# A two-block fp32 network on one core: 32 more tokens by row gathers, dense expert units of 352 columns, and smaller matrices in norms, scores and block inverse

## What is computed

```python
q = (xb @ w_q).reshape(p, PEER_HEADS, 2, PEER_DK_HALF)            # 8 heads, 2 halves of 64
sc = jnp.einsum('phcd,hcnd->phcn', q, sub_keys)                   # 128 keys for each half
top_s, top_i = lax.top_k(sc, PEER_TOPK)                           # 16 of 128, twice
cand_s = (top_s[:, :, 0, :, None] + top_s[:, :, 1, None, :]).reshape(p, PEER_HEADS, kk)
best_s, best_pos = lax.top_k(cand_s, PEER_TOPK)                   # 16 experts for each head
g = jax.nn.softmax(best_s, axis=-1)
act = jax.nn.gelu(jnp.einsum('phkd,pd->phk', expert_u[idx], xb))  # idx: 128 experts for a token
return jnp.einsum('phk,phkd->pd', g * act, expert_v[idx])         # 16384 experts in all
```

## Time and profile before

| | us |
|---|---|
| median of three runs | 1985.86 (1983.73 to 1988.62) |
| the profiled execution | 1983.03 |
| its span, first to last instruction | 1981.3 |
| PE busy | 1834.3 (93%) |
| DVE busy | 1620.6 (82%) |
| POOL busy | 1054.1 (53%) |
| ACT busy | 708.5 (36%) |
| moved by the DMA engines | 440.34 MB |

### The profile page before, as it was taken

One profiled execution on the slowest core, in us unless ns is written; L12 is line 12 of the kernel. 1 busy time (PEld: TensorE's weight loads), 2 busy tenths in 40 slices (PEclk: granted clock), 3 DMA queues, 4 the chain that ended last, 5 costly groups with the idle time before them and its releaser, 6 DMA issues.

```text
span 1981.3 us, 27281 instructions
## 1 busy us (share of the span) xinstructions
PE 1834.3 (93%) x9487; PEld 1581.7 (80%) x9487; DVE 1620.6 (82%) x2566; ACT 708.5 (36%) x1097; POOL 1054.1 (53%) x654
## 2 busy tenths in 40 slices
PE   3997779999999999999999999999999998989885
PEld 1775557999999899999988887878887776778764
DVE  6979967978988798888489999999998868747656
ACT  2343123333333444444333333333334333324441
POOL 1333225488888655555567776767765542343101
PEclk8999779999999999999999999999999999999988
DMA  8241342499889789888999999999994222200011
GB/s 344 88 159 64 128 149 74 137 315 315 308 314 314 258 280 325 300 308 299 317 348 356 353 356 353 349 356 351 363 352 146 75 77 63 73 12 1 2 55 52
DMA packets 160805, 440.34 MB, mean 222 GB/s; under 512 B 13648, under 2 KB 63952, under 8 KB 157648
## 3 DMA queue, kind: packets, MB, share of 16 engines
q1 hardware_dynamic: 65296, 254.71, 36.7%
q0 software_dynamic: 36864, 134.23, 17.9%
q10 hardware_dynamic: 58560, 50.34, 7.7%
HBM read 386.80 MB, written 52.43 MB: 222 GB/s over the span
## 4 chain that ended last, share of the span: by engine, by line
PE 68%; DVE 18%; issue 4%; POOL 4%; ACT 3%; DMA 2%; ACTq 0%; SPq 0%; DVEq 0%; POOLq 0%; PEldq 0%
PE PS L911 30%; PE PS L1078 24%; PE PS L1041 4%; PE PS L1104 4%; POOL w_lo L804 3%; DVE arena L1676 2%; DVE arena L1635 2%; DVE arena L1842 1%; ACT w_hi L1277 1%; PE PS L926 1%; POOL arena L852 1%; PE PS L1002 1%; DMA arena<-in_expert_u_rows,arena 1%; DMA xres<-in_x 1%; DVE arena L1774 1%
## 5 line engine op out<-in xcount | busy, mean ns | idle before, releaser
L804 POOL TENSOR_TENSOR w_lo<-raw,w_hi 128x1024 fp32r<-128x1024 f32 x300 | 725.0, 2417 | 757.7 <-ACT w_hi L1277 756.5
L1277 ACT ACTIVATE w_hi<-raw 128x1024 fp32r<-128x1024 f32 x332 | 351.9, 1060 | 973.4 <-PE PS L911 609.7
L911 PE MATMUL PS<-act_hi,w_hi 128*128 128x384 f32 (+1 forms) x1632 | 603.9, 370 | 37.3 <-DVE act_lo L1648 12.2
L911 PE MATMUL PS<-act_hi,w_lo 128*128 128x384 f32 (+1 forms) x1632 | 588.4, 361 | 0.0
L911 PE MATMUL PS<-act_lo,w_hi 128*128 128x384 f32 (+1 forms) x1632 | 587.5, 360 | 0.0
L911 PEld LDWEIGHTS PS<-act_hi,w_hi 128*128 128x128 f32 x1632 | 311.8, 191 | 91.7 <-issue 25.3
L911 PEld LDWEIGHTS PS<-act_lo,w_hi 128*128 128x128 f32 x1632 | 312.0, 191 | 26.4
L911 PEld LDWEIGHTS PS<-act_hi,w_lo 128*128 128x128 f32 x1632 | 312.6, 192 | 24.3 <-issue 1.4
L1078 PE MATMUL PS<-w_hi,act_hi 128*128 128x512 f32 x768 | 301.3, 392 | 5.6 <-ACT arena L1398 3.0
L1078 PE MATMUL PS<-w_lo,act_hi 128*128 128x512 f32 x768 | 300.2, 391 | 0.0
L1078 PE MATMUL PS<-w_hi,act_lo 128*128 128x512 f32 x768 | 299.9, 390 | 0.0
(11 more groups left out here) (317 smaller groups left out, 1962.7 us busy)
## 6 DMA issues: line engine op xcount, KB each, us to landing
raw<-in_expert_u SPq DMA_DIRECT2D x128, 512.0 KB
raw<-in_expert_v SPq DMA_DIRECT2D x128, 512.0 KB
raw<-in_w_in SPq DMA_DIRECT2D x52, 512.0 KB
arena<-in_w_ada SPq DMA_DIRECT2D x24, 1024.0 KB, 7.1
gel_d<-arena ACTq DMA_DIRECT2D x64, 384.0 KB
gates_d<-arena ACTq DMA_DIRECT2D x12, 2048.0 KB
arena<-gates_d SPq DMA_DIRECT2D x32, 768.0 KB, 7.1
arena<-gel_d SPq DMA_DIRECT2D x32, 768.0 KB
```

The costliest lines, as they stand in the source:

```text
L804: pool.tensor_tensor(w_lo[:, k % SPLIT, :], raw[:, k % RAW, :], w_hi[:, k % SPLIT, :].bitcast(F32), ALU.subtract).then_inc(lo_split, 1)
L911: mm = pe.matmul(PS[:, bank, 0:n_tok], w[:, k % SPLIT, c * P:(c + 1) * P], x[:, c, 0:n_tok], start=(i == 0 and n == 0), stop=(i == KC - 1 ...
L1277: act.activation(w_hi[:, k % SPLIT, :], raw[:, k % RAW, :], ACT.Copy).then_inc(hi_split, 1)
```

## The change

Constants: `TD` = 384 stays for routing and the V stage, the dense units of the U stage have `TU` = 352 columns. The last 32 tokens of block 2 (`XT`) gather too: each stands on four partitions (`REP`), 32 fetches (`XS`) bring its 128 rows, and 32 row dots give `xdots`. Their gelu is multiplied into the routing weight of these tokens, and the V stage's gelu columns for them are ones. `N1`, `N2` become 82 and 126, the dots in the first part 76, those in the second 52 and 32. `own_ps` is overwritten with the 32 tokens' values at group 44 (`SWAP`), when the first 128 dots are done.

```diff
-TB_ORDER = (3, 0, 1, 2)
+TB_ORDER = (3, 2, 0, 1)
+REP = 4
+XT = P // REP
+XS = SLOTS // REP
+TU = TD - XT
+US = SLOTS + XS
...
-        N1 = 75
-        N2 = 122
+        N1 = 82
+        N2 = 126
...
-        DOTS_A, DOTS_B = 72, 51
+        DOTS_A, DOTS_B = 76, 52
+        SWAP, GELU = 44, 86
...
-        DOTS_IN_U = [(TD // GROUP) * d // DOTS_B for d in range(DOTS_B)]
+        DOTS_IN_U = [SWAP * d // DOTS_B for d in range(DOTS_B)] + [SWAP + 3 + (GELU - SWAP - 4) * d // XS for d in range(XS)]
...
-                linear(U_EU + u, u, u % 2, n_tok=TD)
+                linear(U_EU + u, u, u % 2, n_tok=TU)
...
                 for g in GATES_IN[k]:
+                    if g == SWAP:
+
+                        pe.wait_ge(hsum_ready, 2)
+                        pe.wait_ge(rows_used, SLOTS)
+                        for c in range(KC):
+                            mm = pe.transpose(PS[:, 6 + c // 4, (c % 4) * P:(c % 4 + 1) * P], hsum2[:, c, :], ident[:, :])
+                        mm.then_inc(htok_ps, 1)
                     gate_group(g)
```

The one-hot matrices are made by one comparison of 128x512 and four operations of 128x128 with two scalars, in place of 128x1024 and 128x512. The gelus of the dots move from unit 126 to group 86:

```diff
-                chain.link(v.tensor_tensor(hot[:, n, :, :],
-                                           numbers.unsqueeze(1).unsqueeze(1).to_broadcast([P, GROUP, 2, P]),
...
-                v.tensor_tensor(hot[:, n, 1, :], hot[:, n, 1, :],
-                                weight_ps[:, at].unsqueeze(2).to_broadcast([P, GROUP, P]), ALU.mult).then_inc(hot_ready, 1)
+                chain.post(v.tensor_tensor(hot[:, n, 0, :], numbers.unsqueeze(1).to_broadcast([P, GROUP, P]),
+                                           routeT[:, 0, at].unsqueeze(2).to_broadcast([P, GROUP, P]), ALU.is_equal))
+                for i in range(GROUP):
+                    t = GROUP * g + i
+                    chain.post(v.tensor_scalar(hot[:, t % ONEHOT, 1, :], numbers, routeT[:, 1, t:t + 1], routeT[:, 2, t:t + 1],
+                                               ALU.is_equal, ALU.mult))
```

Scores: keys without zeros, one matmul for each half of 64 rows, four in the q units and twelve behind the first twelve (`N0`) units of the U stage:

```diff
-                    mm = pe.matmul(PS[:, 3 + n % 2, 256 * e:256 * e + 256], qT[:, 2 * hp + e, tb * P:(tb + 1) * P],
-                                   keys[:, 2 * hp + e, :], start=True, stop=True)
+                    for c in range(2):
+                        own = slice(64 * c, 64 * c + 64)
+                        mm = pe.matmul(PS[:, 3 + c, P * e:P * e + P], qT[own, 2 * hp + e, tb * P:(tb + 1) * P],
+                                       keys[own, 2 * hp + e, :], start=True, stop=True)
...
+            for u in range(N0):
+                if u >= 2:
+                    pe.wait_ge(gelu_done, u - 1)
+                linear(U_EU + u, u, u % 2, n_tok=TU)
+                scores(len(SCORED_AFTER) + u)
```

Head norms: the squares' sums come out as 128 tokens x 8, the root and the reciprocal are taken there, ACT spreads the result to 64 columns for each head, and PE turns it back:

```diff
+            def head_sum(i):
...
+                for q in range(TB):
+                    mm = pe.matmul(PS[:, 6 + index % 2, 2 * q:2 * q + 2], sq[:, n % 2, q * P:(q + 1) * P], pair,
+                                   start=True, stop=True)
...
+            def head_spread(i):
...
+                for q in range(TB):
+                    mm = pe.matmul(PS[:, 3 + i % 2, q * P:(q + 1) * P], tmp[:, i % 2, q * P:(q + 1) * P], ident[:, :],
+                                   start=True, stop=True)
...
+                v.reciprocal(hinv[:, i % 2, :], hrms[:, i % 2, :]).then_inc(rinv_ready, 1)
```

In `ada`, PE takes the second four of the eight chunks of parts 2 and 3 (16 matmuls of one column each), parts 4 and 5 come later in DVE's and PE's lists, and the first convolution keeps its partial sums on PSUM:

```diff
-        ADA_AFTER = {3: 4, 5: 5, U_OUT + 1: 6, U_OUT + 2: 7, U_OUT + 3: 8, U_OUT + 4: 9, U_Q + 2: 10, U_Q + 4: 11}
+        PE_SHARE = (2, 3)
+        ADA_AFTER = {5: 4, 7: 5, U_OUT + 1: 6, U_OUT + 2: 7, U_OUT + 3: 8, U_OUT + 4: 9, U_Q + 2: 10, U_Q + 4: 11}
...
-                for c in range(KC):
+                for c in range(4 if h in PE_SHARE else KC):
...
-                    pe.wait_ge(xc_ready, g + 1)
+                    pe.wait_ge(xc_ready, (2, 4, 4, 4)[g])
```

Block inverse: D and its transpose are kept as two diagonal blocks of 64x64 for each head, levels 0 to 5 work on these alone, and the last level joins them. The masks go to 24:

```diff
+            def quarters(name, *pieces):
+
+                b = bank(*name)
+                wait_free(pe, *name)
+                for h in range(GH):
+                    for to, lhs, rhs in pieces:
+                        mm = pe.matmul(PS[to, b, 64 * h:64 * h + 64], lhs[:, h, :], rhs[:, h, :], start=True, stop=True)
                 full(mm, *name)
...
-                    chain.post(v.tensor_tensor(DTm[:, tb, :], DTm[:, tb, :], PS[:, bank("xt", n, tb), :], ALU.subtract))
...
+                        chain.post(v.tensor_tensor(dt, dt, turned_x, ALU.subtract))
...
-                        chain.post(v.tensor_tensor(Dm[:, tb, :], Dm[:, tb, :], PS[:, bank("x", n, tb), :], ALU.subtract))
+                        chain.post(v.tensor_tensor(d, d, PS[:, bank("x", n, tb), 0:256], ALU.subtract))
```

More of the change, by code:

```diff
@@ L465, in build @@
         rows_known = sem("rows_known")
-        rows_got = [sem(f"rows_got{i}") for i in range(RING + 2)]
+        rows_got = [sem(f"rows_got{i}") for i in range(RING)]
         rows_used = sem("rows_used")
@@ L550, in unit_bank, with piece_used @@
             return n % 4 if n < 12 else n % 2 if n < 32 else (n + 1) % 2
+        def piece_used(i):
+            if i % 2 and i // 2 in PE_SHARE:
+                return ada_used_pe, PE_SHARE.index(i // 2) + 1
+            return ada_used, sum(1 for n in range(i + 1) if not (n % 2 and n // 2 in PE_SHARE))
         def cvp(n):
@@ L972, in _ @@
                     if Y_SUM[i] == u:
-                        squares(8 + i, 1, 1 + i, halves)
-            for i in range(8):
-                if Y_SUM[i] == 20:
-                    squares(8 + i, 1, 1 + i, halves)
+                        head_sum(i)
+                    if Y_SPREAD[i] == u:
+                        head_spread(i)
+            head_spread(3)
+            head_sum(6)
+            head_spread(4)
+            head_sum(7)
+            for i in range(5, 8):
+                head_spread(i)
             for c in range(8):
@@ L1015, in _ @@
                     scores(SCORED_AFTER[c])
-            pe.wait_ge(q_sb, 8)
-            for n in range(len(SCORED_AFTER), TB * 4):
-                scores(n)
             pe.wait_ge(hsum_ready, 1)
@@ L1341, in _ @@
                     if Y_SUM[i] == u:
-                        root(1 + i, 64)
+                        head_root(i)
+                    if Y_SPREAD[i] == u:
+                        spread(i)
                 for i in range(8):
@@ L1357, in _ @@
             square(15, y[:, Y_ORDER[7], :])
-            for i in range(5):
-                y_upper(i)
-            root(7, 64)
-            y_upper(5)
-            root(8, 64)
-            y_upper(6)
-            y_upper(7)
+            spread(3)
+            y_upper(0)
+            y_upper(1)
+            head_root(6)
+            spread(4)
+            y_upper(2)
+            head_root(7)
+            spread(5)
+            y_upper(3)
+            spread(6)
+            y_upper(4)
+            spread(7)
+            for i in range(5, 8):
+                y_upper(i)
             for c in range(8):
@@ L1374, in score_copy @@
                 act.wait_ge(score_ps, n + 1)
-                act.activation(S[:, 4 * n:4 * n + 4, :].rearrange("p a b -> p (a b)"), PS[:, 3 + n % 2, :],
-                               ACT.Copy).then_inc(score_sb, 1)
+                own = S[:, 4 * n:4 * n + 4, :].rearrange("p (e c) b -> p e c b", c=2)
+                for c in range(2):
+                    ins = act.activation(own[:, :, c, :], PS[:, 3 + c, 0:2 * P].rearrange("p (e b) -> p e b", e=2), ACT.Copy)
+                ins.then_inc(score_sb, 1)
             for c in range(8):
@@ L1383, in _ @@
                     score_copy(SCORED_AFTER[c])
-            for n in range(len(SCORED_AFTER), TB * 4):
-                score_copy(n)
             def expert_act(u, k, r=None, first=False):
@@ L1695, in _ @@
             chain.link(v.tensor_tensor(ada[:, 0:16], PS[:, 5, 0:16], col("bada", 0, 16), ALU.add))
+            chain.link(v.tensor_tensor(ada[:, 8:16], PS[:, 5, 48:56], ada[:, 8:16], ALU.add))
             chain.link(v.scalar_tensor_tensor(out=gain1, in0=ada[:, 8:16], scalar=1.0, in1=col("n1", 0, 8),
@@ L1927, in _ @@
                     dve.wait_ge(htok_ps, 1)
+                if tb == GT - 1:
+                    own = slice(P - XT, P)
+                    f = row_f[own, :]
+                    chain.link(v.tensor_scalar(f, routed_sb[tb][own, 1, :], float(N_KEYS), None, ALU.mult))
+                    chain.link(v.tensor_tensor(f, f, routed_sb[tb][own, 0, :], ALU.add))
+                    for r in range(REP):
+                        chain.post(v.tensor_copy(row_x[XT * r:XT * r + XT, :], f[:, XS * r:XS * r + XS]))
+                    chain.wait()
+                    dve.nop().then_inc(rows_known, 1)
             assert place == [POINTS, DOTS_A]
```

290 lines of the change are left out of this document (199 added, 91 removed).

## The result

The changed kernel takes 2025.0 us (median of 4 runs, 2021.1 to 2028.2), the kernel before 1985.6 in runs beside it: 1.0196 of it, with an interval of 1.0169 to 1.0222. It is slower by 39 us where 51 us faster was forecast. The forecast put the first U unit at 306, the first routing transposes of PE (which the gate part begins with) at 643, the last group at 923 and the V stage at 953; they came at 339.1, 697.4, 1009.8 and 1042.3 us. So 33 us were lost ahead of the U stage, 22 in its first part, some 32 in the gate part and 2 behind it.

The account below looks back on a forecast made before the run. PE bounds the U and V stages and inverse, with DMA engines and DVE close; DVE bounds the front. -34 -1 -2 +0 -14 = -51: 1932 us profiled, 1935 against the median; own range 1922 to 1948, 8 in 10 within 1905 to 1960.

Parts of the forecast that it names:

- Gate part: U stage's second part: 280 us against 282.2 before, set by DMA work, with about 2 us won.
- a one-hot group is 0.60 for 512 elements and 4 x 0.27: Gate part, DVE's need: 1.7 us a group, with 84 dots of 1.2 in all 264 us.
- the DMA engines' 279.4 us of work: Gate part: raw loads, gathers, gelu and gate stores sum to 279.4 us, more than PE's time, so they set it.
- First part: U stage's first part: units of 3.84 us, with scores and POOL's delays 336.5 us; net gain 1 with scores.
- Front: Everything ahead of the U stage: 34 us won by fewer reciprocals and ada multiply-adds on DVE, ends 24 to 39.
- The later ends it: Front: the later of DVE's bound 181.5 and PE's unit 19 at 165 plus 13 us tail, 178; 35 won.
- hides behind DVE's reciprocal: Front: PE's share of ada, 32 one-column matmuls, costs nothing, so PE's first unit starts 6.4 us earlier.
- Scores: Scores ahead of and in the U stage: 0.63 us each in place of 0.92; 12 behind U units cost 7.6.
- Gap before the V stage: From last group to V stage: 30 us as before, PE standing for 22; no change, ends -3 and +3.
- Inverse: Block inverse: products in quarters take 0.65 us in place of 0.89; 14 us won, ends 0 and 30.
- Rival 2: Gate part gets longer through POOL, fetches waiting for dots hold splits and PE: 300 us, total 1955; chance 0.18.
- Rival 4: Slower: gate part's 84 row gathers take 2.0 us each in place of 1.35, stage 334; priced 1990, chance 0.03.

Follow-up runs that it names:

- run 6: The changed kernel with a group's one-hots made by two wide operations as before, the weights in PSUM; 2012.6 us (1.0143).
- run 13: The changed kernel with only 16 of 128 partitions of each gate store written, V stage output left out; 2014.2 us (1.0142).
- the mended kernel: The changed kernel with row numbers in PSUM, two wide one-hot operations with weights in PSUM, masks early, table exchange at group 52; 2010.6 us (1.0121).
- run 11: The mended kernel without the 32 extra gathers and dots, the 52 old dots over 80 groups; 1966.6 us (0.9905).
- run 3: The changed kernel without the 32 dot products of the extra tokens, their row gathers kept; 2022.8 us (1.0192).
- run 4: The changed kernel without the 32 extra dot products and without their 32 gathers; 2007.3 us (1.0115).
- run 5: The changed kernel with the intermediate row numbers of the 32 tokens in PSUM in place of SBUF; 2020.2 us (1.0175).
- run 14: The kernel before with changed front and block inverse, all of ada's multiply-adds on DVE again, none on PE; 1968.9 us (0.9912).
- run 1: The changed kernel with POOL's iota, distances and masks moved behind the split of the first q unit; 2023.3 us (1.0188).
- run 7: The kernel before with the change of the block inverse alone; 1973.1 us (0.9947).
- run 2: The changed kernel with a group's one-hots made by two wide operations, the weights in SBUF; 2073.5 us (1.0444).

## Why the prediction was wrong, point by point

*Gate part (forecast 280, ends 256 to 300; measured 312 by the same events, 302 from one-hots to one-hots).* **The step that failed is DVE's need: "a one-hot group is 0.60 for 512 elements and 4 x 0.27", 1.7 us, and 264 in all.** The eight operations of the earlier trace rows, 0.27 each, were of the same kind and size; the new ones follow one another at 0.32 to 0.33 (1.36 us for four, with the last one's end), the compare takes 0.60 to the next start, as forecast, and each group also waits for its own results before it is handed to PE (the 0.19 of idle time ahead of the dot). A group takes 2.15 us, 0.45 more than forecast: 96 x 0.45 = 43 us. With that, DVE's sum is 302, and DVE holds the part (runs 6 and 13). The same sum shows why the change of the one-hots was itself a loss: the two wide operations need 1.86. A second term was short too, and would have shown with the right price for DVE: the DMA engines' 279.4 us of work was right (0.88 of 312.5 us is 275, a gather 1.43 where 1.35 was taken), but the step from this work to a stage of 280, the engines full all the way, failed. Their share in the half behind group 44 is 0.84, in the changed kernel and in run 6, where the stage still waits for gathers and stores; in the mended kernel the part takes 291 us, 303 by the forecast's events. PE's 256.5 was near: in run 11 PE is busy 247.9 of 253.5 us.

*Dots.* Not forecast was that the exchange of the table presses 52 old dots into 44 groups. There DVE needs 44 x 2.15 + 52 x 1.14 = 154 us, and 154.0 is what this half takes; in run 11, where DVE has 29 dots there, it takes 119.2. So leaving the 32 new dots out can give nothing there, and behind group 44 the gathers and stores hold the time (runs 3 and 4).

*First part (forecast 336.5; measured 358.4 by the same events, 363 to the first one-hots).* PE's 24 matmuls of 352 columns do take 3.84 us, but from gelu to gelu units take 3.8 and 4.1 in turn, 3.95 in the mean, where units of 384 took 4.16. The narrower unit gives 0.21, not 0.33. PE stops for POOL's split:

```profile
425.47 0.43 PE L951 MATMUL PS<-act_hi,w_hi 128*128 128x352 f32 x1 [0.64 <-POOL w_lo L840]
```

A split takes ACT's 1.06 and POOL's 2.40 behind the unit that frees its buffer, and a fetch ahead of it 0.96 more; in a unit of 3.84 no slack is left. That is argued from the durations, no run changed it. A score was priced at 0.63 and its matmuls take 0.65; but unit and score together take 4.70, so each of the 12 costs 0.86. In sum: 70 units at 0.11 more, 8; scores 3; the stop at the row numbers, 7 between the two traces and 5 in the median (run 5); the rest, some 4 of the 22, lies in single stops and in the routing's end.

*Front (forecast 34, ends 24 to 39; measured 7.2).* **The step that failed is the tail and PE's bound, 178, in "The later ends it".** DVE's reciprocals fell from 20 to 12, as expected, and its last split of `y` was forecast near 182. It is at 209.7 to 210.4. PE's bound was 8 us short before any chain of waits began: unit 17 (counted from 0) ended at 162.4, where the forecast's end of unit 19 at 165 wants 154. The first unit had come 3 us later than forecast, and from unit 14 on the units start 6.8 us apart, as before, not 5.49, because a head's sum stands between them (0.80 and a gap of 0.29 in the chain above). Then PE's list has spreads and sums ahead of each unit, and these wait for ACT and DVE: the last two units end at 188.3, 26 us later, where 11 are two units' work. 10 of it lie between the units, and 5 are lower clock: the units take 7.58 and 8.39 us in place of 5.49. The granted clock was 1.00 from 158 to 165 us, 0.51 from 165 to 172 and 0.50 from 178.9 to 185.5, thus 1.2 in place of 2.4 GHz; each time it fell in a gap between two units, of 5.6 and 4.3 us, in which PE had only a head's spread and sum. The tail behind them took 22, not 13. These three, 8 + 15 + 9, are the 32 us from 178 to 210.4. In the tail the spread and the sum of a head take PE 2.08 and 1.51 us (from 192.5 to 206 us the granted clock is 0.50), where they take 1.16 and 0.80 at the full clock. A second failed term is that PE's share "hides behind DVE's reciprocal": its 64 records take 0.15 to 0.21 us each, 11.6 us, and DVE waits 6.6. Of the 6.4 us forecast, 3.3 came. And 6.5 us won at the end of `y` were 4.9 at the end of the q units (332.8 against 337.7), where DVE's `ada` work lies between; no run separates that. Which of the terms is worth how much of the 7.2 is not shown by runs either, but by one trace, save for PE's share (run 14).

*Scores.* They gave 1.7 us (12.0 before, 12 x 0.86 now), not the 4.4 of the sum. From PE's last q unit to its first U unit the way is 6.3 us, where 14.4 before less the 12.0 of scores leave 2.4; with the masks early it is 3.7 (run 1).

*Gap before the V stage (forecast 30.2 us, as before; measured 32.3, and 38.2 us both times from the last group of one-hots).* Right within its ends. The gate store took 14.21 in place of 10.47 and the raw load 7.52 in place of 9.21. PE's stop there was forecast at 22 us and is 22.8, so this cost was known; that it takes nearly all that the narrow units win was not said.

*V stage (no change; 530.4 against 528.8).* Right.

*Inverse (forecast 14, 102 us long, 0.65 a product; measured 12.4, 103.9 long).* Right within the measurement. Three products that follow one another took 1.61 us, 0.54 each, so the fixed 0.21 of the forecast does not show in each of them, and stops between them take it back, PE being busy 90.6 of 103.9 us (chain of waits of run 7):

```profile
1784.00 1.61 PE PS L1122 x48
```

*The rivals.* Rival 2 named the symptom, fetches that wait for dots (74.9 us of POOL in the gate part), but took 300 us as its end and POOL as the cause. Rival 4, slower, had the wrong mechanism: row gathers at 2.0 us each, where they took 1.43. No rival let DVE be the bound, though it was named ahead of the sum with 242 of 282 us busy, and the sum left it 16 us from the top. That was the forecast's real fault: of three engines within 10% of each other DVE alone was given no part in the outcome, and its price came from a row without its waits.

## What to carry to other kernels

Where several engines are each near 90% of a stage (here PE 99, DVE 86 and the DMA engines 87% before), taking work from one of them moves the bound by the distance to the next; give every one of them a range, and price its operations with their waits, by start-to-start times. Here the units narrowed by 8% were worth nothing in this arrangement even with their replacement work free, 19 us of it because the last groups had moved close to the end of the stage, and the two small edits elsewhere gave all that was measured. When two limits stand level, leaving out the work of one shows nothing: it takes the runs that remove each, and the halves of the stage looked at apart. A unit that gets shorter also takes the slack out of whoever feeds it.

## What the hardware did that was not expected

- An operation of DVE with its operands in SBUF was held for the whole of POOL's operation: 0.69 us became up to 3.12 (run 2), and 2.55 became 0.30 with one end in PSUM (run 5). The front's multiply-adds take 0.76 and at times 2.78 in both kernels; in the changed kernel the one at 214.86 us stands beside a split that runs from 214.15.
- The last gate store, of the same bytes, took 10.47 us in one kernel and 14.21 in the other, where gathers took 37% of the DMA engines' time beside it and none before.
- Matmuls of one or two columns are not small: the eight records of a head's sum, two columns each, took 0.80 us at the full clock, 0.10 each, where 16 of 128 columns took 1.78, 0.11 each.
